# Reordering three instruction queues at the entry of a seven-product feed-forward block

## The reference

```python
def _finish(x, attn_o, conv_o, w_out, norm_ffn_g, w_gate, w_up, w_down):
    ...
    h = x + mix @ w_out
    hn = rms_norm(h, norm_ffn_g)
    return h + (jax.nn.silu(hn @ w_gate) * (hn @ w_up)) @ w_down
```

## Time and profile before

| | before |
|---|---|
| time, median of 3 runs | 1278.8 us (1278.54 to 1278.9) |
| time of the profiled execution | 1278.54 us |
| its span, first to last instruction | 1276.8 us |
| TensorE matmul busy | 1257.5 us, 98% |
| VectorE busy | 519.9 us, 41% |
| ScalarE busy | 377.6 us, 30% |
| GpSimd busy | 628.6 us, 49% |

### The profile page before, as it was taken

One profiled execution on the slowest core, in us unless ns is written; L12 is line 12 of the kernel. 1 busy time (PEld: TensorE's weight loads), 2 busy tenths in 40 slices (PEclk: granted clock), 3 DMA queues, 4 the chain that ended last, 5 costly groups with the idle time before them and its releaser, 6 DMA issues.

```text
span 1276.8 us, 21896 instructions
## 1 busy us (share of the span) xinstructions
PE 1257.5 (98%) x9082; PEld 1169.2 (92%) x9082; DVE 519.9 (41%) x951; ACT 377.6 (30%) x715; POOL 628.6 (49%) x520
## 2 busy tenths in 40 slices
PE   7999999999999999999999999999999999999997
PEld 7997778989766699999999999999999999999997
DVE  6844313323766522579413131313131313131156
ACT  6000110100577611355232323232323232323323
POOL 3453023323365441042775757575757575757735
PEclk9999999999999999999999999999999999999999
DMA  5546367262111041011211111111111111111203
GB/s 203 185 160 221 108 231 258 100 211 86 50 67 68 1 175 63 1 34 34 67 48 53 47 53 49 52 46 55 46 55 44 57 42 59 41 60 39 78 2 136
DMA packets 38098, 107.99 MB, mean 85 GB/s; under 512 B 4016, under 2 KB 16496, under 8 KB 36208
## 3 DMA queue, kind: packets, MB, share of 16 engines
q1 hardware_dynamic: 38000, 106.60, 24.4%
HBM read 95.73 MB, written 10.85 MB: 83 GB/s over the span
## 4 chain that ended last, share of the span: by engine, by line
PE 90%; DVE 5%; ACT 2%; issue 1%; DMA 1%; SPq 0%; POOL 0%; DVEq 0%; ACTq 0%
PE ps L1156 11%; PE ps L1158 11%; PE ps L1157 11%; PE ps L1190 7%; PE ps L1192 7%; PE ps L1191 7%; PE ps L721 6%; PE ps L723 5%; PE ps L722 5%; PE ps L861 3%; PE ps L906 3%; PE ps L885 2%; PE ps L930 2%; PE ps L931 2%; PE ps L932 2%; PE ps L838 1%
## 5 line engine op out<-in xcount | busy, mean ns | idle before, releaser
L1156 PE MATMUL ps<-combo,w_hi 128*128 128x264 f32 x672 | 191.2, 284 | 0.8 <-ACT evac L1215 0.8
L1158 PE MATMUL ps<-combo,w_lo 128*128 128x264 f32 x672 | 190.8, 284 | 0.0
L1157 PE MATMUL ps<-combo,w_hi 128*128 128x264 f32 x672 | 190.5, 284 | 0.0
L596 POOL TENSOR_TENSOR w_lo<-w_stage,w_hi 128x512 fp32r<-128x512 f32 (+1 forms) x56 | 75.2, 1343 | 193.7 <-ACT w_hi L1215 193.6
L2025 DVE TENSOR_TENSOR resid<-ps,resid 128x352 f32<-128x352 f32 x240 | 125.9, 525 | 103.5 <-PE ps L1192 103.5
L721 PE MATMUL ps<-act_hi,w_hi 128*128 128x352 f32 x480 | 158.5, 330 | 8.5 <-DVE act_lo L1651 8.5
L1190 PE MATMUL ps<-hid,w_hi 128*128 128x352 f32 x504 | 163.0, 323 | 0.7 <-DVE resid L2025 0.7
L1192 PE MATMUL ps<-hid,w_lo 128*128 128x352 f32 x504 | 162.5, 322 | 0.0
L1191 PE MATMUL ps<-hid,w_hi 128*128 128x352 f32 x504 | 162.3, 322 | 0.0
L723 PE MATMUL ps<-act_hi,w_lo 128*128 128x352 f32 x480 | 154.8, 322 | 0.0
L722 PE MATMUL ps<-act_lo,w_hi 128*128 128x352 f32 x480 | 154.7, 322 | 0.0
(11 more groups left out here) (336 smaller groups left out, 2988.4 us busy)
## 6 DMA issues: line engine op xcount, KB each, us to landing
w_stage<-in_w SPq DMA_DIRECT2D x75, 512.0 KB, 3.6
resid<-in_state_k SPq DMA_DIRECT2D x8, 1792.0 KB, 7.5
v_buf<-in_state_v SPq DMA_DIRECT2D x14, 1024.0 KB, 4.9
raw<-in_w SPq DMA_DIRECT2D x22, 512.0 KB, 3.6
resid<-in_xT SPq DMA_DIRECT2D x16, 528.0 KB, 7.8
out_yT<-resid SPq DMA_DIRECT2D x24, 176.0 KB, 1.8
q_d<-out SPq DMA_DIRECT2D x12, 176.0 KB, 4.3
out_kT<-out SPq DMA_DIRECT2D x12, 176.0 KB, 1.9
```

Of the source, the lines that this page charges most:

```text
L596: pool.tensor_tensor(w_lo_row[:, cols_], half_unit(f, product), f32(w_hi_row[:, cols_]), ALU.subtract).then_inc(half_split, 1)
L1156: pe.matmul(out, hi[:, wk], x_hi[:, k, tk], start=(k == 0 and first), stop=False, skip_group_check=not first)
L1157: pe.matmul(out, hi[:, wk], x_lo[:, k, tk], start=False, stop=False, skip_group_check=not first)
L1158: mm = pe.matmul(out, lo[:, wk], x_hi[:, k, tk], start=False, stop=(k == 3), skip_group_check=not first)
```

## The change

Three queues are reordered; no instruction is added, removed or altered.

- GpSimd: `last_weight_sum(2)` goes from behind `second_hidden(1)` to ahead of `weight_low(1, "P3")`.
- ScalarE: in the stretch behind `weight_high(2, "P6")`, the order was `weight_high(1, "P3")`, `hidden_high1(0)`, S4's high parts 2 and 3, `silu_second(1)`, `keep_p1(2)`. It becomes S4's high parts 2 and 3, `hidden_high1(0)`, `keep_p1(2)`, `silu_second(1)`, `weight_high(1, "P3")`. And `keep_u2(2)` goes from ahead of `hidden_high1(1)` to behind `silu_first(2)`, as for the other tiles.
- VectorE: the order was `second_gate(1)`, the two `first_low`, `first_hidden_low1()`, `second_up(1)`, four low parts of S4. It becomes low parts 0 and 1 of S4, the two `first_low`, low parts 2 and 3, `first_hidden_low1()`, `second_gate(1)`, `second_up(1)`.

```diff
@@ gpsimd
             weight_low(1, "P6")
+            last_weight_sum(2)
             weight_low(1, "P3")
             second_hidden(1)
-            last_weight_sum(2)
             weight_low(2, "P5")
@@ scalar
             weight_high(2, "P6")
-            weight_high(1, "P3")
-            hidden_high1(0)
             for k in range(2, 4):
                 combo_high(S4, y12, k, S4_AT[k])
+            hidden_high1(0)
+            keep_p1(2)
             silu_second(1)
-            keep_p1(2)
+            weight_high(1, "P3")
             weight_high(2, "P5")
             hidden_high2(1)
             weight_high(2, "P4")
             weight_high(2, "P3")
-            keep_u2(2)
             hidden_high1(1)
             for f in range(2, FT):
...
                 silu_first(f)
                 if odd:
                     weight_high(f + 1, "P1")
-                if f > 2:
-                    keep_u2(f)
+                keep_u2(f)
@@ vector
             third_weight_sums()
-            second_gate(1)
+            for k in range(2):
+                combo_low(28, y12, S4, k)
             first_low(2, "P7")
             first_low(2, "P6")
+            for k in range(2, 4):
+                combo_low(28, y12, S4, k)
             first_hidden_low1()
+            second_gate(1)
             second_up(1)
-            for k in range(4):
-                combo_low(28, y12, S4, k)
             first_hidden(1)
```

## The result

The changed kernel takes 1286.65 us (median of 4, 1286.33 to 1286.72) against 1278.76 us before: a ratio of 1.0061, with an interval of 1.0044 to 1.0079. It is 7.9 us slower, where 4.7 was forecast and 1284.9 was the upper end of the range. The forecast's direction held, its size did not. The profiled execution took 1286.63 us with a span of 1284.8.

A forecast was written before the change was run, and what follows sets the result against it. The prediction took the time to be TensorE's queue plus its gaps: +3.34 + 2.86 - 0.53 - 1.00 = +4.67 us on the profiled 1278.54 us gave 1283.2 us, with a range of 1281.8 to 1284.9.

The forecast's parts named there:

- gap in front of P7: TensorE, tile 2: P7 waits for the later `second_gate(1)` and starts at 602.90 instead of 599.56, +3.34 us.
- round trip in front of P5: TensorE, tile 2: P5 waits for `keep_u2(2)`, now behind a chain that starts from P3 of tile 1, +2.86 us.
- old gaps: TensorE: the stop inside P3 of tile 1 and the wait before P5 of tile 2 close, -0.53 and -1.00 us.
- GpSimd's share: VectorE's queue ahead of `second_gate(1)`: `last_weight_sum(2)` on GpSimd slows it once, by 1.13 us.
- bound of 1.70: Upper bound of GpSimd's share: its instruction slows two VectorE instructions by the mean excess of 0.85 us each.
- rival 1: The GpSimd instruction doesn't meet VectorE's queue ahead of `second_gate(1)`: +3.5 us, 1282.1 us; chance 0.12.
- sum of +4.67: Whole kernel: two new TensorE gaps less two closed ones, +3.34 + 2.86 - 0.53 - 1.00 us, giving 1283.2 us.
- rival 2: TensorE's clock falls in the new gaps: +6.2 us, 1284.7 us for one; +7.7, 1286.2 for both; chance 0.12.
- sign of being wrong: TensorE behind a gap: a matmul pace over 0.12 us would show the prediction wrong.
- The price: TensorE behind a gap: one clock fall costs 1.5 us, read off ten slow matmuls at the kernel's start.
- rival 2's figure for two falls: TensorE: if both new gaps bring the clock down, +7.7 us, 1286.2 us.

The follow-up runs named there:

- e6: The changed kernel with `second_gate(1)` back ahead of the low parts of S4 on VectorE: 1282.06 us, ratio 1.0024.
- e7: The kernel before with the move of `keep_u2(2)` alone: 1281.19 us, ratio 1.0021.
- e3: The changed kernel with `last_weight_sum(2)` back behind `second_hidden(1)` on GpSimd: 1283.1 us, ratio 1.0038.
- e9: The changed kernel with small matmuls of ones, eight in the gap before P7 of tile 2 and four before P5: 1283.13 us, ratio 1.0035.
- e4: The changed kernel with `keep_u2(2)` back in front of `hidden_high1(1)` on ScalarE: 1282.68 us, ratio 1.0032.
- e14: The changed kernel again, unchanged, for more executions, against the kernel before: 1285.93 us, ratio 1.0058.
- e8: The kernel before with `last_weight_sum(2)` ahead of `weight_low(1, "P3")` and `second_up(1)` behind the four low parts of S4: 1277.84 us, ratio 0.9992.
- e10: The changed kernel with both `last_weight_sum(2)` and `keep_u2(2)` at their old places: 1281.98 us, ratio 1.0021.
- e2: The changed kernel with eight small matmuls of ones in the gap in front of P7 of tile 2: 1284.68 us, ratio 1.0049.

## Why the prediction was wrong

**The reading of the queues was right.** The gap in front of P7 was forecast as 3.34 and is 3.38; e6 cut it to 0.5 by moving `second_gate(1)` alone. The round trip in front of P5 was forecast as 2.86 and is 2.84; e7 made it with `keep_u2(2)` alone. The old gaps of 0.53 and 1.00 closed. GpSimd's share, 1.13, is 1.11 in the trace and by e3. The bound of 1.70 was not needed, and rival 1 fell. The sum of +4.67 is met by e9, the changed kernel without its clock loss: 1283.13 us against the forecast 1283.2.

**The step that failed is rival 2,** the clock, which the sum put at nothing. The prediction says: "So nearly 4 us of idling brought it down", and from it: "Gaps of 3.3 and 2.9 us are shorter than 4 us". One fall, at the end of the kernel, was read as the least idling that does it, while it only shows that so much suffices. That the gaps of the old kernel left no trace bounds it from below, and these are 1.1 us and shorter. Between 1.1 and 4 us the trace of before said nothing, both new gaps were there, and the rival got 0.12. The prediction's own sign of being wrong, a pace over 0.12 us behind a gap, came true. In the traces the clock fell 1.9 us (e4), 2.1 (e14) and 2.6 (the changed kernel) after the last matmul had ended. Over all executions it came to (gaps from matmul start to matmul start):

| gaps, us | kernel | executions | with a clock loss |
|---|---|---|---|
| 1.1, 0.6 | before | 27 (run with e6) | none; 1278.1 to 1279.4 |
| 0.9 | e8 | 11 | none |
| filled to 1.0 and 1.5 of idling | e9 | 5 | none |
| 2.4, 1.0 | e10 | 11 | 7 |
| 3.0, 0.7 | e7 | 11 | 6 |
| 3.0, 0.6, 0.3 | e6 | 11 | 7 |
| 2.4, 3.0 | e3 | 4 | 2 |
| filled to 1.0 of idling, 3.0 | e2 | 4 | 4 |
| 3.5, 1.0 | e4 | 5 | 4 |
| 3.5, 3.0 | changed | 10 | 10 |

From e10 down the counts are of executions that lie 0.5 us or more above the sum of waits. The fall itself is seen in the traces of the changed kernel, e2, e4, e7, e10 and e14; for the other executions it is inferred. They have a mean clock of 0.998 or less, but so have some executions of before with no loss, so the times carry the counts. The kernel before scatters up to 0.7 us above its median, and one execution of e7 (1281.19 us, 0.6 above) may be no fall; all the others lie about 1.0 or more above. The gap of 3.0 us had no slow matmuls behind it in the two traces of the changed kernel, each time 12 us or more behind a fall, and 26 in e2, without one. About half the executions of e6 and e7 also went through such a gap unharmed, so whether the earlier fall protects is open.

The Trainium skill, TensorE: Matmul & The Clock Gate, Part 1, says that an array that has idled falls to half clock, and that the point at which the clock changes differs from run to run of one kernel. The executions of e10, e6 and e7, one program with two outcomes each, fit this. The prediction cited the page for the fall and not for the chance in it.

**The price was mis-sized too.** 1.5 us was read off the first matmuls, which were slow from 7.97 us to somewhere between 11.04 and 11.70. In the changed kernel the slow stretch is 6.1 us long and costs 2.77; in e7 and e10 it is shorter and costs 1.5. The range took in one fall at 1.5, so it is this price that put the result outside it. With 4.67 and 2.77 the forecast would have been 1286.0, within 0.7 of what was measured. That rival 2's figure for two falls, 1286.2, lies closer still is luck: only one gap brought the clock down, at nearly twice the price.

## What to carry to other kernels

An engine with 41% of busy time can still be the late one: before moving an instruction back in a queue, find who waits for it and count what now stands ahead of it. Where a job waits for a copy, check that the copy's own queue doesn't wait for the job right ahead of it; that round trip was worth 2.9 us here. Here gaps on TensorE of 2.4 us and more lost the clock in about half of the executions or more, and idling of up to 1.5 us in none; nothing between was tried. Such a gap is to be priced at its length plus one slow stretch, 1.5 to 2.8 us here, as the likely case, and one sighting of a limit tells only on which side of it one point lies.

## What the runs showed of the hardware

- The clock can fall behind the gap. In e7 the matmuls ran 0.12 apart again from 611.58, and the clock fell in the stretch from 612 to 613; e10 shows the same behind 602.22. In the changed kernel it fell inside the gap.
- At the lower clock a 128x128 by 128x264 matmul follows the last at 0.22 us, at the upper one at 0.12.
- Small matmuls in the gap, whose results nobody reads, kept the clock up (e9). They won 3.5 us over the changed kernel, or 2.8 over its executions in e14, almost without shortening a wait.
- VectorE instructions with both inputs in SBUF and GpSimd instructions hinder each other: four took 5.87 us beside three of GpSimd and 2.55 with GpSimd idle (e8), which is 1.11 per GpSimd instruction. `last_weight_sum(2)` itself took 1.63 us beside them and 1.29 alone (e3). `first_hidden(1)` and `first_gate(2)`, with one input in PSUM, took 0.71 and 0.70 in the kernel before, as usual, although GpSimd worked beside them:

```profile
609.03 1.28 POOL L596 TENSOR_TENSOR w_lo<-w_stage,w_hi 128x512 fp32r<-128x512 f32 x1
```

The Trainium skill, SBUF — State Buffer, "Who interferes with whom", has this rule, and these rows agree with it in kind. The price was 1.11 us, 0.2 less than a whole GpSimd instruction.
